# Two blocks of a transformer on one core: part of the modulation product moved from TensorE to VectorE

## The reference, cut to what matters

```
sc  = jax.nn.silu(c)        # one row of 2048
scc = jax.nn.silu(c_ctx)    # another
for i in range(2):
    shift, scale, gate    = jnp.split(sc  @ mod_w[i] + mod_b[i], 3, axis=-1)   # mod_w[i]: 2048 x 6144
    cshift, cscale, cgate = jnp.split(scc @ mod_w[i] + mod_b[i], 3, axis=-1)
```

## Time and profile before

| | |
|---|---|
| median of 3 runs | 2440.16 us (2439.88 to 2441.19) |
| the profiled execution, its time | 2443.28 us |
| its span | 2441.2 us |
| PE busy | 2421.8 us (99%) |
| DVE busy | 1488.0 us (61%) |
| ACT busy | 1189.6 us (49%) |
| POOL busy | 127.6 us (5%) |
| DMA | 432.54 MB, 177 GB/s over the span |

### The profile page before, as it was taken

One profiled execution on the slowest core, in us unless ns is written; L12 is line 12 of the kernel. 1 busy time (PEld: TensorE's weight loads), 2 busy tenths in 40 slices (PEclk: granted clock), 3 DMA queues, 4 the chain that ended last, 5 costly groups with the idle time before them and its releaser, 6 DMA issues.

```text
span 2441.2 us, 31070 instructions
## 1 busy us (share of the span) xinstructions
PE 2421.8 (99%) x11777; PEld 1921.6 (79%) x11777; DVE 1488.0 (61%) x2043; ACT 1189.6 (49%) x1758; POOL 127.6 (5%) x84
## 2 busy tenths in 40 slices
PE   9999999999999999999999999999999999999999
PEld 7887777787777777888888888888887887878877
DVE  6644445564545555667676767875556476664865
ACT  6644344653544444556656666424425344253462
POOL 0000000000000000013211111001300000000000
PEclk9999999999999999999999999999999999999999
DMA  8578887737787777565333333555435444354444
GB/s 286 172 213 268 252 270 254 242 118 257 243 272 232 254 242 246 186 242 128 104 95 98 95 97 92 183 187 165 130 111 157 129 121 146 114 153 130 129 128 148
DMA packets 285440, 432.54 MB, mean 177 GB/s; under 512 B 20855, under 2 KB 100109, under 8 KB 284301
## 3 DMA queue, kind: packets, MB, share of 16 engines
q1 hardware_dynamic: 284140, 422.56, 55.6%
q10 hardware_dynamic: 1184, 8.41, 0.9%
HBM read 428.79 MB, written 2.12 MB: 177 GB/s over the span
## 4 chain that ended last, share of the span: by engine, by line
PE 94%; DVE 2%; ACT 2%; DMA 1%; issue 1%; POOL 0%; SPq 0%; ACTq 0%; DVEq 0%
PE ps L826 67%; PE ps L1238 13%; PE ps L901 3%; PE ps L1219 2%; PE ps L1014 1%; PE ps L877 1%; PE ps L979 1%; PE ps L1346 1%; PE ps L1364 1%; PE ps L1191 1%; PE ps L999 1%; DMA ring<-in_att_w_out 1%; ACT ring_hi L1483 1%; DMA ring<-in_att_w_in 0%; PE ps L1355 0%
## 5 line engine op out<-in xcount | busy, mean ns | idle before, releaser
L2018 DVE TENSOR_TENSOR ring_lo<-ring,ring_hi 128x1024 fp32r<-128x1024 f32 (+2 forms) x576 | 694.1, 1215 | 625.1 <-ACT ring_hi L1483 620.9
L1483 ACT CAST ring_hi<-ring 128x1024 fp32r<-128x1024 f32 (+2 forms) x598 | 619.6, 1040 | 893.6 <-PE ps L826 499.6
L826 PE MATMUL ps<-ring_hi,act_hi 128*128 128x512 f32 (+2 forms) x1272 | 505.9, 398 | 2.3 <-ACT proj L1562 1.2
L826 PE MATMUL ps<-ring_hi,act_lo 128*128 128x512 f32 (+2 forms) x1272 | 490.8, 386 | 0.0
L826 PE MATMUL ps<-ring_lo,act_hi 128*128 128x512 f32 (+2 forms) x1272 | 489.6, 385 | 0.0
L826 PE MATMUL ps<-ring_hi,features_hi 128*128 128x512 f32 x1152 | 457.5, 397 | 1.0 <-issue 0.8
L826 PE MATMUL ps<-ring_hi,features_lo 128*128 128x512 f32 x1152 | 449.2, 390 | 0.0
L826 PE MATMUL ps<-ring_lo,features_hi 128*128 128x512 f32 x1152 | 448.6, 389 | 0.0
L826 PEld LDWEIGHTS ps<-ring_hi,act_hi 128*128 128x128 f32 x1272 | 239.1, 188 | 71.7 <-issue 20.9
L826 PEld LDWEIGHTS ps<-ring_hi,act_lo 128*128 128x128 f32 x1272 | 238.8, 188 | 49.4
L826 PEld LDWEIGHTS ps<-ring_lo,act_hi 128*128 128x128 f32 x1272 | 239.4, 188 | 43.5
(11 more groups left out here) (291 smaller groups left out, 2459.0 us busy)
## 6 DMA issues: line engine op xcount, KB each, us to landing
ring<-in_mod_w SPq DMA_DIRECT2D x192, 512.0 KB, 4.7
ring<-in_att_w_in SPq DMA_DIRECT2D x128, 512.0 KB, 3.8
ring<-in_ev_w_in SPq DMA_DIRECT2D x104, 512.0 KB, 4.7
ring<-in_od_w_in SPq DMA_DIRECT2D x96, 512.0 KB, 5.0
ring<-in_lru_w_in SPq DMA_DIRECT2D x64, 512.0 KB, 4.1
ring<-in_ev_w_out SPq DMA_DIRECT2D x40, 512.0 KB, 4.2
ring<-in_lru_w_out SPq DMA_DIRECT2D x40, 512.0 KB, 4.2
ring<-in_od_w_out SPq DMA_DIRECT2D x36, 512.0 KB, 4.8
```

Of the source, the lines that this page charges most:

```text
L826: mm = pe.matmul(PS[:, bank, 0:n], a, w[:, k - k0, :], start=(k == k_first and j == 0), stop=(k == k_last and j == 2))
L1483: act.copy(high(U, n), raw(U, n)).then_inc(s_hi, 1)
L2018: dve.tensor_tensor(out=low(U, n), in0=raw(U, n), in1=high(U, n).bitcast(F32), op=ALU.subtract).then_inc(s_lo, 1)
```

## The change

Chunks 3, 7, 11 and 15 of the 19 (`SUMMED`) are no longer multiplied by TensorE. For each of their k-tiles and both conditioning vectors VectorE multiplies the raw 512 columns with a per-partition scalar from `cond_t` and adds them to an accumulator in a free part of `proj` (`summed_mod`). When the 16 k-tiles are in, TensorE sums over the partitions with a stationary slice of `OZ` that holds one column of ones, into the partitions of bank 3 in which that chunk's rows belong, in two halves of 256 columns for each row; this stands in `fill_mod` ahead of the first pair behind the chunk's last unit. The units of these chunks stay in the ring, and SP waits for VectorE's step count `s_am` before it reloads such a slot. The order by hand changes with it: 16 pairs are gone, and 32 single summed units stand behind given projection units.

```
-    return range(ROUND_AT[r], ROUND_AT[r + 1])
+    return [m for m in range(ROUND_AT[r], ROUND_AT[r + 1]) if m not in SUMMED]
...
-def with_mod(units, pairs, before_head=False):
+def with_mod(units, pairs, before_head=False, summed=()):
...
         out += units[k:k + 1]
+        if k in summed:
+            out.append(("sum_mod", next(SUMMED_UNITS)))
...
-EV_SECOND = with_mod(chunk_units("ev_b", [11]), 4)
-EV_TURNS = lay_turns(0, [(MEM_EV, 0, (3, 4, 4, 3), (1, 2, 1, 1)), (MEM_EV, 1, (3, 4, 4, 3), (1, 2, 1, 1)), (MOBA, 0, (3, 4, 4, 3), (1, 2, 1, 1)),
-                         (MOBA, 1, (3, 4, 3, 3), (1, 2, 1, 1)), (MOBA, 2, (3, 4, 3, 2), (1, 1, 1, 1)), (MOBA, 3, (3, 4, 2, 2), (1, 1, 1, 1))],
+EV_SECOND = with_mod(chunk_units("ev_b", [11]), 3, summed=(5, 7))
+EV_TURNS = lay_turns(0, [(MEM_EV, 0, (3, 4, 4, 3), (1, 1, 1, 1), ((0,), (0,), (0,), ())), (MEM_EV, 1, (3, 4, 4, 3), (1, 1, 1, 1), ((0,), (0,), (0,), ())),
+                         (MOBA, 0, (3, 4, 4, 3), (1, 1, 1, 1), ((), (0,), (0,), ())), (MOBA, 1, (3, 4, 3, 3), (1, 1, 1, 0), ((0,), (0,), (), ())),
+                         (MOBA, 2, (3, 4, 3, 2), (1, 1, 1, 0), ((0,), (0,), (), ())), (MOBA, 3, (3, 4, 2, 2), (1, 1, 1, 0), ((0,), (0,), (), ()))],
...
-OUT_MID = with_mod(OUT_C1[4:] + ..., 8)
+OUT_MID = with_mod(OUT_C1[4:] + ..., 6, summed=(4, 7, 10, 13, 16, 19))
-OD_FIRST = with_mod(chunk_units("od_b", [0])[2:], 2)
-OD_SECOND = with_mod(chunk_units("od_b", [2]), 2)
-OD_THIRD = with_mod(chunk_units("od_b", [8]), 3)
-OD_TURNS = lay_turns(10, [(SWA[j], i, (1, 3, 2, 1), (0, 1, 1, i % 2)) for j in range(2) for i in range(4)]
+OD_FIRST = with_mod(chunk_units("od_b", [0])[2:], 1)
+OD_SECOND = with_mod(chunk_units("od_b", [2]), 2, summed=(2,))
+OD_THIRD = with_mod(chunk_units("od_b", [8]), 2, summed=(1,))
+OD_TURNS = lay_turns(10, [(SWA[j], i, (1, 3, 2, 1), (0, 1, 1, 0), ((), (0,) if 4 * j + i < 6 else (), (0,) if 4 * j + i < 2 else (), ())) for j in range(2) for i in range(4)]
...
+        OZ = SC[:, 140:139 + 2 * MOD_COLS]
...
+                    if RING[back][0] == "sum_mod":
+                        m, j = divmod(RING[back][1], 8)
+                        sp.wait_ge(s_am, 32 * SUMMED.index(m) + 4 * (j + 1))
...
+                if u in SUM_ADDED:
+                    n = SUM_ADDED.index(u)
+                    at_row = 2 * (SUMMED[n] - ROUND_AT[r])
+                    pe.wait_ge(s_am, 32 * (n + 1))
+                    for w in range(2):
+                        for half in range(2):
+                            g, cols = 64 * w + 32 * half, slice(half * CHUNK // 2, (half + 1) * CHUNK // 2)
+                            pe.matmul(PS[g:g + MOD_COLS, MB, cols], OZ[:, MOD_COLS - 1 - at_row - w:2 * MOD_COLS - 1 - at_row - w],
+                                      summed_rows(n)[w][:, cols], start=False, stop=False)
...
+            def summed_mod(u):
+
+                m, j = divmod(u, 8)
+                n = SUMMED.index(m)
+                U = POS["sum_mod", u]
+                if n and j == 0:
+                    dve.wait_ge(s_wused, POS["mod", SUM_ADDED[n - 1]] + 1)
+                dve.wait_ge(s_w[U % SLOTS], landed(U))
+                for k in range(2 * j, 2 * j + 2):
+                    for w in range(2):
+                        rows, by, acc = raw(U)[:, k % 2 * CHUNK:(k % 2 + 1) * CHUNK], CS[:, 2 * k + w:2 * k + w + 1], summed_rows(n)[w]
+                        if k == 0:
+                            ins = dve.tensor_scalar(acc, rows, by, None, ALU.mult)
+                        else:
+                            dve.wait_ge(s_am, 32 * n + 2 * k + w - 1)
+                            ins = dve.scalar_tensor_tensor(out=acc, in0=rows, scalar=by, in1=acc, op0=ALU.mult, op1=ALU.add)
+                        ins.then_inc(s_am, 1)
...
                     lo_to(split_behind(U - 1))
+                    if unit[0] == "sum_mod":
+                        summed_mod(unit[1])
```

More of the change, by code:

```diff
@@ L182 @@
 N_MOD = 19
+SUMMED = (3, 7, 11, 15)
 N_HOST = 2
@@ L209, in __init__ @@
         self.even = heads in (MEM_EV, MOBA, MLA)
-MOD_UNITS = iter(range(8 * N_MOD))
-def with_mod(units, pairs, before_head=False):
+MOD_UNITS = iter([8 * m + j for m in range(N_MOD) if m not in SUMMED for j in range(8)])
+SUMMED_UNITS = iter([8 * m + j for m in SUMMED for j in range(8)])
+def with_mod(units, pairs, before_head=False, summed=()):
     out, n = [], len(units)
@@ L231, in lay_turns @@
     turns, at = [], 0
-    for j, (heads, i, counts, pairs) in enumerate(plan):
+    for j, (heads, i, counts, pairs, summed) in enumerate(plan):
         gaps = []
-        for count, p in zip(counts, pairs):
-            gaps.append(with_mod(units[at:at + count], p, True))
+        for count, p, behind in zip(counts, pairs, summed):
+            gaps.append(with_mod(units[at:at + count], p, True, behind))
             at += count
@@ L252 @@
                      chunk_units("ev_b", EV_FILL) + chunk_units("uq", range(3), 2))
-MLA_TURNS = lay_turns(6, [(MLA, 0, (1, 2, 1, 0), (0, 0, 0, 0)), (MLA, 1, (1, 2, 1, 0), (0, 0, 0, 0)), (MLA, 2, (1, 1, 1, 0), (0, 0, 0, 0)),
-                          (MLA, 3, (1, 1, 1, 0), (0, 0, 0, 0))],
+NONE = ((), (), (), ())
+MLA_TURNS = lay_turns(6, [(MLA, 0, (1, 2, 1, 0), (0, 0, 0, 0), NONE), (MLA, 1, (1, 2, 1, 0), (0, 0, 0, 0), NONE),
+                          (MLA, 2, (1, 1, 1, 0), (0, 0, 0, 0), NONE), (MLA, 3, (1, 1, 1, 0), (0, 0, 0, 0), NONE)],
@@ L255 @@
                       chunk_units("ev_b", [8]) + [("ev_out", u) for u in (8, 9, 4, 5, 6, 7)])
 OUT_C1 = [("ev_out", 10 + u) for u in range(4, 10)]
-OUT_MID = with_mod(OUT_C1[4:] + [("ev_out", 10 * c + u) for c in range(2) for u in range(4)] + [("ev_out", u) for u in range(20, 32)], 8)
+OUT_MID = with_mod(OUT_C1[4:] + [("ev_out", 10 * c + u) for c in range(2) for u in range(4)] + [("ev_out", u) for u in range(20, 32)], 6,
+                   summed=(4, 7, 10, 13, 16, 19))
 OUT_LAST = with_mod([("ev_out", 38), ("ev_out", 39)], 1)
-OD_FIRST = with_mod(chunk_units("od_b", [0])[2:], 2)
@@ new lines @@
+OD_SECOND = with_mod(chunk_units("od_b", [2]), 2, summed=(2,))
+OD_THIRD = with_mod(chunk_units("od_b", [8]), 2, summed=(1,))
+OD_TURNS = lay_turns(10, [(SWA[j], i, (1, 3, 2, 1), (0, 1, 1, 0), ((), (0,) if 4 * j + i < 6 else (), (0,) if 4 * j + i < 2 else (), ())) for j in range(2) for i in range(4)]
+                     + [(DIL, 0, (1, 3, 1, 1), (0, 1, 1, 0), NONE), (DIL, 1, (1, 2, 1, 1), (0, 1, 1, 0), NONE), (DIL, 2, (1, 2, 1, 1), (0, 1, 1, 0), NONE),
+                        (MEM_OD, 0, (1, 1, 1, 1), (0, 1, 1, 0), NONE), (MEM_OD, 1, (1, 2, 1, 0), (0, 0, 0, 0), NONE)],
@@ L265 @@
                      chunk_units("od_b", OD_FILL) + chunk_units("od_c", [0]))
-assert next(MOD_UNITS, None) is None
+assert next(MOD_UNITS, None) is None and next(SUMMED_UNITS, None) is None
 RING = []
@@ L322 @@
     SPLIT_BEFORE.append(sum(_made))
-    if _name in ("mod", "gate_mod", "host_mod"):
+    if _name in ("mod", "sum_mod", "gate_mod", "host_mod"):
         LO_BY.append(None)
@@ L354, in used_by @@
 def used_by(U):
-    return 2 if U + 1 < len(RING) and RING[U + 1][0] in ("gate_mod", "host_mod") else 1
+    return 2 if U + 1 < len(RING) and RING[U + 1][0] in ("sum_mod", "gate_mod", "host_mod") else 1
 def split_behind(U):
@@ L398 @@
 ROWS_BY = {next(s for s in SPLIT_UNITS if s > POS["mod", round_end(r)]): r for r in range(N_ROUND)}
-SUMS_BY = {max(s for s in SPLIT_UNITS if s < POS["mod", round_end(r) + 1]): r for r in range(N_ROUND - 1)}
+SUMS_BY = {max(s for s in SPLIT_UNITS if s < POS["mod", 8 * ROUND_AT[r + 1]]): r for r in range(N_ROUND - 1)}
 SUMS_BY[POS[OD_TURNS[-1].gaps[1][1]]] = N_ROUND - 1
 assert len(ROWS_BY) == len(SUMS_BY) == N_ROUND and all(r <= s for r, s in zip(sorted(ROWS_BY), sorted(SUMS_BY)))
+SUM_ADDED = []
+for _m in SUMMED:
+    _r = next(r for r in range(N_ROUND) if ROUND_AT[r] <= _m < ROUND_AT[r + 1])
+    _u = next(u for name, u in RING[POS["sum_mod", 8 * _m + 7]:] if name == "mod")
+    assert _u % 2 == 0 and 8 * ROUND_AT[_r] < _u <= round_end(_r)
+    SUM_ADDED.append(_u)
+assert sorted(set(SUM_ADDED)) == SUM_ADDED
+assert all(POS["mod", u] < POS["sum_mod", 8 * m] for u, m in zip(SUM_ADDED, SUMMED[1:]))
 def evicted(stage, c):
@@ L581, in build, with summed_rows @@
         CZ = SC[:, 0:(KT + 1) * MOD_COLS - 2]
+        OZ = SC[:, 140:139 + 2 * MOD_COLS]
+        def summed_rows(n):
+            H, c = (HE, 8) if SUM_ADDED[n] <= round_end(ROUNDS_BEFORE_MLA - 1) else (HO, 7)
+            return [H[:, w, c * CHUNK:(c + 1) * CHUNK] for w in range(2)]
         SQX, SQL, SQC, SQG = (SC[:, j:j + 8].rearrange("p (t c) -> p t c", t=TT) for j in (72, 56, 64, 80))
@@ L628, in build @@
         s_gm, s_gsum = map(sem, ("gate_mod_step", "gate_summed"))
+        s_am = sem("summed_mod_step")
         s_hm, s_hs, s_hcol = map(sem, ("hosted_mod_step", "hosted_mod_summed", "hosted_mod_ready"))
@@ L695, in weights @@
                 c, j = divmod(u, units_of(stage))
-                if stage == "mod":
```

(9 more changed lines are left out.)

2 lines of the change are left out of this document (removed).

## The result

| | before, same chip | after |
|---|---|---|
| median of 10 runs | 2440.26 us (2439.24 to 2441.46) | 2447.02 us (2443.79 to 2448.84) |
| ratio | | 1.0027, 95% interval 1.0018 to 1.0036 |
| profiled execution, its span | 2443.28, 2441.2 us | 2448.84, 2446.8 us |

What follows compares the result with a forecast made beforehand. PE, busy 99% of the span, was taken as the bound. 18.2 us saved less 2.2 for added groups and 7.0 of lateness gave 9.0 us, so a median of 2431.2 us, range 2423.5 to 2439.

Steps and rivals of the forecast that it cites:

- 18.2 us: PE time saved by 16 pairs gone: ten ahead of projections at 1.18 us, six ahead of transposes at 1.06.
- The added groups: Four groups of four 256-column products on PE, each ahead of a pair: 0.55 us each, 2.2 in all, ends 1.6 and 4.2.
- the rule on equal tiling modes: Tiles of one mode run independently, so added groups cost their stream alone; without it 1.06 us each, 4.2 in all.
- OUT_MID: Each sum needs a low part whose load waits for the sum before; PE 1 us late, ends 0 and 5.
- finished sums: PE's four waits for them, ahead of mod units 18, 52, 84 and 116: 0.3 us, ends 0 and 2.
- the lateness in EV_SECOND: Sums made one behind the other, with low parts and loads waiting, make PE late at three turn 0 units: 4 us.
- The sign that I had named for the slots: PE's waits for `ring_lo` should grow from 7 to about 14 us; staying at 7 would mean the slot's part was wrong.
- A beat of the clock is no case: No clock drop expected: PE idled 3 us in 2340 to 2400 us at clock 1.00, and the forecast waits are shorter.
- 7.0 us in all: Sum of PE's lateness from modulation slots now freed by VectorE, in EV_SECOND, turn 1, OUT_MID and other places; ends 0 and 20.
- Rival 2: The slot held by VectorE becomes the ring's step, in the turns too: 12 to 15 us of lateness, 2437 us; chance 0.16.
- rival 3: Slower: with landings of about 6 us throughout, 0.6 to 0.7 us lost for each of 32 sums, 2448 us; chance 0.06.

Runs made afterwards that it cites:

- e6: e5 with VectorE's sums taken into the bank by two products of 512 columns a group instead of four of 256: 2432.98 us, ratio 0.9966 to the kernel before.
- e7: The kernel before with 20 linked memsets by VectorE ahead of its copy of the key columns: 2457.27 us, ratio 1.0063.
- e1: The changed kernel with VectorE's copy of the key columns moved ahead of the last unit of EV_SECOND: 2440.56 us, ratio 1.0000 to the kernel before.
- e5: The changed kernel with VectorE's copy of the key columns moved two units ahead, before the last two of EV_SECOND: 2440.59 us.
- e9: e6 with VectorE making a unit's sums before the low halves of the units ahead of it: 2428.27 us, ratio 0.9951 to the kernel before.
- e12: e9 with four products of 256 columns a group and eight small products behind TensorE's wait for the key columns: 2429.00 us, ratio 0.9955 to the kernel before.
- e4: The kernel before with sixteen more products of 8 columns (64 instructions) at TensorE's start: 2454.39 us, ratio 1.0058.
- e2: The changed kernel with twelve more products of 8 columns (48 instructions) at TensorE's start: 2443.02 us, ratio 1.0009 to the kernel before.
- e3: The changed kernel with both the copy moved as in e1 and the twelve small products of e2: 2436.80 us, ratio 0.9985 to the kernel before.
- e11: The kernel before with 10 small products (40 instructions) at TensorE's start: 2444.27 us in one run.
- e10: The kernel before with 24 small products (96 instructions) at TensorE's start: 2450.06 us in one run.

## Why the prediction was wrong

**What held.** 480 records, 32 new ones, 120 + 8 steps of VectorE at 745 and 480 ns. By starts of the same products, a pair gone in front of a projection shortened PE's stream by 1.18 us (1.07 to the first product behind it, 0.11 in the step after that) and one in front of transposes by 1.06: 18.2 us stand. The added groups are 4 x 0.44 = 1.8 us where I took 2.2; without the rule on equal tiling modes beside that term it would have been 1.06 a group, so 0.44 agrees with it. OUT_MID lost 1.0 us in one wait, as taken, and PE waited 0.4 us for finished sums (I took 0.3).

**The step that failed: the lateness in EV_SECOND, "4 us, ends 0 and 7".** It is 12.6 us: 10.5 more in one wait (11.0 against 0.5) and some 2.1 in a slow clock. The sign that I had named for the slots, waits for `ring_lo` that grow from 7 to 14 us, did not come (5.1 us in 7 waits of the weight loads, where the earlier trace rows have 6.8 in 8; e6, without the copy's wait, has 9.7 in 11): the lateness stood in the wait for the copy. The rows used were of a unit's load, cast and use, and I reckoned the delays of products from their low parts. That the second unit's sums would wait for a low part whose load had waited for the first was right; they came at 201.6 to 204.3 us. What I left out is what stands behind that unit in VectorE's own program: the copy for which PE waits without any lead (PE waits 0.5 us for it already in the kernel before; e7). Rows 9 do not show that copy. e1 and e5 take the wait away.

**"A beat of the clock is no case" failed with it.** It rested on 3 us of idle time in 60. After 11.0 us in one piece the clock was at its lower level, 0.50 until 209.4 us; after 3.4 us in one piece in e1, 0.51 for 3.5 us; after 1.1 and 2.9 us close together at the loop, 0.66 over 10 us. e6, e9 and e12 have no such wait and a clock of 1.00 at both places.

**The step that was missing: where the code lies.** No part of the prediction looked behind 1010 us. Fewer instructions ahead of a loop moved its body in the code, most likely over a block's border, and 7.7 us went in its second pass. e4 shows the loss without the change, e2, e3, e6 and e12 the change without the loss. That the ten fetches are the loop's own blocks is inferred from their number, their time and the records between them; the profile doesn't say what a fetch holds.

**The rest of the lateness came out near its size, for a reason that was half right.** I had 7.0 us in all, from slots that VectorE holds; with the copy and the loop mended e6 loses 5.1 us to it, in turns 0 and 1, and e9 shows the mechanism: less the 3.0 us of the sums than their place behind low parts that themselves wait for loads.

**The account.** Forecast 2431.2. The loop 7.7 and the copy's 12.6 in place of 4 make 2447.5, and 2447.0 was measured. That it comes out so near is in part luck: outside the two losses, the starts of the same products show lateness of 0.8 us at 283, 0.8 at 321, 1.1 at 623 and 1.4 at 785 us, some 4 in all where 3.0 are left of the forecast, while two waits of the kernel before, 1.3 us at 1147 and 1.1 at 2344 us, are not there in the kernel after, for no reason that the forecast had. With both mended e6 lies 8.2 us under its kernel before, where the forecast was 9.0, with up to 1.7 us paid for its wider products. Rival 2 had the right mechanism in turns 0 and 1 and at few places behind them: from 300 us on the changed kernel has one wait for `ring_lo`, of 1.0 us, and one of 1.3 us at 785 us that the profile puts down to "issue":

```profile
782.33 1.05 ACT L1520 CAST ring_hi<-ring 128x1024 fp32r<-128x1024 f32 x1 [4.96 <-DMA ring<-in_od_w_in]
783.67 1.04 ACT L1520 CAST ring_hi<-ring 128x1024 fp32r<-128x1024 f32 x1 [0.30 <-DMA ring<-in_od_w_in]
784.62 0.36 ACT L1620 COPY arena<-ps 128x256 f32<-128x256 f32 x1
```
```profile
785.09 1.02 PE L1016 MATMUL ps<-arena 64*128 64x128 f32 x8 [1.29 <-issue]
```

PE's products of a head wait for ScalarE's copy, which stands behind two casts that wait for loads; e1 and e5 have this wait too, the kernel before and e6 do not. That there are so few places speaks against rival 3, whose loss would lie along all 32 sums. Its condition did not come either: the loads of `ring` land in 4.8 us on the median in 200 to 460 us and in 5.4 in 545 to 625 us, not in 6.

What stays open: the changed kernel's runs spread over 5 us, those of the kernel before beside them over 2, but nearly 5 in the 27 runs beside e1 to e4. Kernels with the loop's ten fetches show spreads of 2 to 5 us and kernels without them of 1 to 5, so these do not explain it. Open too is how many blocks are held and when one is fetched ahead: the runs fit eight, and none of them measures it.

## What to carry to other kernels

When a unit of work is given to another engine, read that engine's program on behind it to the next thing for which the bottleneck waits, and ask how much lead that thing has; here a copy of 0.42 us with none cost 12.6 us. Work whose end frees a buffer belongs ahead of work that waits for a buffer. A change of some tens or a few hundred instructions ahead of a long hardware loop can cost or give 7.7 us by its place alone: look at the count of instruction fetches and for waits on "issue" behind the branch before the data flow is blamed, and try the same kernel with a few instructions more or less.

## What was not expected of the hardware

- A loop of 1565 TensorE records runs its second pass without one fetch, or with ten and 7.7 us more, as its place changes by 24 instructions one way or 32 the other (e11, e4 and e10: 240 records from the last fetch to the branch, good; 28 to 30, bad; 40, good). In the kernel before and in nine others 6.1 blocks were run again without a fetch.
- Twelve small products of 8 columns (24 records) at the start took 4.9 us, 0.2 us a record, as much as a record of 512 columns in the later stream: padding ahead of the first rows is not cheap. The same product at 194 us in e12 takes half of that, 0.11 us a record (16 records from 193.73 us, the next instruction at 195.54). That the clock is at its lower level at the start would explain it, but the profile gives 1.00 there.
- After the wait of 11 us products started 0.43 us apart instead of 0.23 until 209.4 us, 4.7 us behind the wait's end. The same came behind a wait of only 3.4 us in e1, for 3.5 us.
